# Nineteen weight chunks: high parts by rounding transfers of GpSimd's queue, low parts one chunk later, and ScalarE copying all transposed probabilities

## The reference

```python
h = rms_norm(x, norm1_g)
rx, rgate, q, kc, vc, ks, vs, kw, vw, nsa_g, mg_rnn, mg_attn = split(h @ w_in)
hr = rg_lru(causal_dwconv(rx, ...), ...)          # gated linear recurrence, two tanh gates
y_rnn = (hr * gelu(rgate)) @ w_rnn_out
y_attn = nsa(q, kc, vc, ks, vs, kw, vw, nsa_g, ...) @ w_attn_out   # three branches: compressed, selected, window
x = x + (sigmoid(mg_rnn) * y_rnn + sigmoid(mg_attn) * y_attn) @ w_out
```

## Time and profile before

| what | value |
|---|---|
| time, median of 3 runs | 812.38 us (812.19 to 812.41) |
| profiled execution, span | 810.6 us |
| PE busy | 799.6 us (99%) |
| DVE busy | 599.4 us (74%) |
| ACT busy | 487.0 us (60%) |
| POOL busy | 27.1 us (3%) |
| DMA | 143.79 MB, mean 177 GB/s |
| high parts by ACT (L629) | 127 of 1877 ns mean |
| low parts by DVE (L1074) | 127 of 2247 ns mean |

### The profile page before, as it was taken

How to read it: one execution, slowest core, us unless ns; L and a number is a source line. 1 busy time by engine, 2 the same in 40 slices (tenths; PEclk the granted TensorE clock), 3 DMA queues, 4 the chain that set the end, 5 groups by cost and what they waited for, 6 DMA issues and landing times.

```text
span 810.6 us, 11913 instructions
## 1 busy us (share of the span) xinstructions
PE 799.6 (99%) x4813; PEld 693.2 (86%) x4813; DVE 599.4 (74%) x773; ACT 487.0 (60%) x738; POOL 27.1 (3%) x38
## 2 busy tenths in 40 slices
PE   8999999999999999999999999999999999999996
PEld 7889998888888888988888888888888988888885
DVE  6774698998957986897878778877777665655556
ACT  6555598877757454765666566546755654544552
POOL 1102000000000000000000000020110000000000
PEclk9999999999999999999999999999999999999999
DMA  8446432342434674456455555764453655555441
GB/s 337 164 156 251 170 126 104 118 155 73 151 119 159 229 288 156 156 188 227 160 206 174 201 197 175 256 237 147 146 196 121 211 201 196 174 219 191 161 152 52
DMA packets 22630, 143.79 MB, mean 177 GB/s; under 512 B 2608, under 2 KB 3248, under 8 KB 8240
## 3 DMA queue, kind: packets, MB, share of 16 engines
q1 hardware_dynamic: 20880, 137.72, 48.3%
q10 hardware_dynamic: 1696, 5.31, 1.8%
HBM read 141.97 MB, written 1.05 MB: 176 GB/s over the span
## 4 chain that ended last, share of the span: by engine, by line
PE 93%; ACT 3%; DVE 2%; DMA 1%; issue 1%; DVEq 0%; SPq 0%; ACTq 0%
PE PS L1748 19%; PE PS L1752 10%; PE PS L1801 10%; PE PS L1802 10%; PE PS L1805 10%; PE PS L1735 5%; PE PS L1736 4%; PE PS L1740 4%; PE PS L2115 3%; PE PS L1764 2%; PE PS L2094 2%; PE PS L1858 1%; PE PS L1892 1%; PE PS L2119 1%; PE PS L1869 1%; PE PS L2065 1%
## 5 line engine op out<-in xcount | busy, mean ns | idle before, releaser
L1074 DVE TENSOR_TENSOR WL<-RAW,WH 128x2048 fp32r<-128x2048 f32 (+2 forms) x127 | 285.1, 2247 | 31.1 <-ACT WH L629 31.0
L629 ACT ACTIVATE WH<-RAW 128x2048 fp32r<-128x2048 f32 (+2 forms) x127 | 238.2, 1877 | 47.0 <-PE PS L1805 25.7
L1490 DVE TENSOR_TENSOR HLS<-PS,HLS 128x512 f32<-128x512 f32 x46 | 31.7, 689 | 92.7 <-ACT HLS L977 92.7
L1748 PE MATMUL PS<-CHL,WH 128*128 128x512 f32 x352 | 87.9, 392 | 0.0
L1735 PE MATMUL PS<-BHL,WH 128*126 128x256 f32 (+1 forms) x336 | 83.6, 287 | 0.0
L977 ACT ACTIVATE HLS<-PS 128x512 f32<-128x512 f32 x46 | 27.4, 595 | 90.7 <-PE PS L1752 86.3
L1736 PE MATMUL PS<-BHL,WH 128*126 128x256 f32 (+1 forms) x336 | 81.8, 282 | 0.0
L1748 PE MATMUL PS<-BHL,WH 128*128 128x512 f32 x320 | 79.9, 392 | 0.0
L1748 PEld LDWEIGHTS PS<-CHL,WH 128*128 128x128 f32 x352 | 63.9, 189 | 11.8
L1802 PE MATMUL PS<-WH,AHL 128*128 128x512 f32 x176 | 68.8, 391 | 0.0
L1801 PE MATMUL PS<-WH,AHL 128*128 128x512 f32 x176 | 68.7, 390 | 0.0
(11 more groups left out here) (313 smaller groups left out, 1311.1 us busy)
## 6 DMA issues: line engine op xcount, KB each, us to landing
RAW<-in_w_stream SPq DMA_DIRECT2D x108, 1024.0 KB, 4.8
RAW<-in_w_stream SPq DMA_DIRECT2D x11, 1008.0 KB, 4.9
RAW<-in_w_stream SPq DMA_DIRECT2D x8, 704.0 KB, 4.5
WF<-in_w_stream SPq DMA_DIRECT2D x2, 1024.0 KB, 5.4
LN<-in_ln ACTq DMA_DIRECT2D x2, 1024.0 KB, 5.2
WF<-in_w_stream SPq DMA_DIRECT2D x4, 294.0 KB, 3.6
X<-in_x SPq DMA_DIRECT2D x2, 512.0 KB, 4.2
RAW<-in_w_stream SPq DMA_DIRECT2D x2, 512.0 KB, 6.8
```

The costliest lines, as they stand in the source:

```text
L629: eng.activation(WH[:, c % NSLOT, 0:CHUNKS[c][2]], raw(c), ACT.Copy).then_inc(w_hi, 1)
L1074: eng.tensor_tensor(WL[:, c % NSLOT, 0:CHUNKS[c][2]], raw(c), f32(WH[:, c % NSLOT, 0:CHUNKS[c][2]]), ALU.subtract).then_inc(w_lo, 1)
L1490: eng.tensor_tensor(HLS[:, n % 4, :, :], PS[:, bank:bank + 2, 0:TOK], HLS[:, n % 4, :, :], ALU.add)\
L1748: eng.matmul(PS[:, bank, :], wh, HL[:, k, :, :].rearrange("p a t -> p (a t)"), start=(k == 0), stop=False)
```

## The change

Nineteen of the chunks that have two parts, from chunk 17 to chunk 39 (all but the "ri" chunks), form the list CAST. For these:

- POOL issues a transfer from HBM straight into the slot of WH; source and target differ in type (float32 and the rounded type), so the transfer rounds. It waits until PE has finished chunk c - 3, and until the transfer two before it has landed. Two semaphores in turn say that it landed. SP loads RAW as before, so these chunks are read from HBM twice.
- ACT no longer rounds them. PE and DVE wait for the transfer in place of ACT's semaphore (`wait_high`).
- DVE makes the low part of chunk c + 1 at the top of iteration c, behind the maxima and ahead of the unit's weights, where it made that of chunk c + 2 in mid-iteration. It also waits for RAW itself.
- ACT copies both PSUM banks of the transposed probabilities, in one instruction of 128 x 1024; DVE's `unit_pt` is gone, and one semaphore takes the place of two.
- In the feed-forward parts two sets of semaphores become one; what is waited for stays the same.

```diff
+CAST = [c for c in range(AT[("ri", 0)] + 1, AT[("ao", 3)] + 1) if CHUNKS[c][3]]
+HI_NO = [sum(1 for b in range(c) if CHUNKS[b][3] and b not in CAST) for c in range(NCH)]
...
+        def wait_high(eng, c):
+            if c in CAST:
+                n = CAST.index(c)
+                eng.wait_ge(wh_in[n % 2], 16 * (n // 2) + 16)
+            else:
+                eng.wait_ge(w_hi, HI_NO[c] + 1)
...
@@ gpsimd
             power(crs[0:NKV * CP, :], css[0:NKV * CP, :], 1, HD, EPS, kc_rstd)
+            for n, c in enumerate(CAST):
+                eng.wait_ge(chunk_done, c - NSLOT + 1)
+                if n >= 2:
+                    eng.wait_ge(wh_in[n % 2], 16 * (n // 2))
+                source = A_w[OFFS[c]:OFFS[c + 1]].rearrange("(p n) -> p n", p=P)
+                eng.dma_start(WH[:, c % NSLOT, 0:CHUNKS[c][2]], source).then_inc(wh_in[n % 2], 16)
@@ scalar, split
-                if c >= NCH or not CHUNKS[c][3]:
+                if c >= NCH or not CHUNKS[c][3] or c in CAST:
@@ scalar, unit_pt
-                eng.activation(PT[:, u % 2, 0, :, :].rearrange("p h q -> p (h q)"), PS[:, 4, :], ACT.Copy)\
-                   .then_inc(pt0_copied, 1)
+                eng.activation(PT[:, u % 2, :, :, :].rearrange("p a h q -> p (a h q)"),
+                               PS[:, 4:6, :].rearrange("p a q -> p (a q)"), ACT.Copy).then_inc(pt_copied, 1)
@@ vector, split
-                s = SPLIT_NO[c]
-                eng.wait_ge(w_hi, s + 1)
+                wait_high(eng, c)
+                if c in CAST:
+                    eng.wait_ge(raw_in[ARRIVAL[c][0]], 16 * (ARRIVAL[c][2] + 1))
@@ vector, window
-                u = unit_at(w - 2)
-                if u is not None:
-                    unit_pt(u)
@@ vector, loop over c
-                if c and CHUNKS[c - 1][0] == "ri" and c - 1 != SPLIT_AHEAD or c == UNIT_FIRST:
+                if c + 1 in CAST:
                     split(c + 1)
...
-                if CHUNKS[c][:2] not in SUMS_FIRST and kind != "ri" and c != W0 and c + 1 != UNIT_FIRST or c == SPLIT_AHEAD:
+                if CHUNKS[c][:2] not in SUMS_FIRST and c + 2 not in CAST and c != W0:
                     split(c + 2)
```

More of the change, by code:

```diff
@@ L437, in two_block_program @@
             "pct_done", "pct_copied", "qk_done", "nb_ready", "exp_done", "p_ready", "t_done"))
-        pt0_copied, pt1_copied, pv_done, o_hi, o_lo, rnn_g, la_ready = (sem(n) for n in (
-            "pt0_copied", "pt1_copied", "pv_done", "o_hi", "o_lo", "rnn_g", "la_ready"))
+        pt_copied, pv_done, o_hi, o_lo, rnn_g, la_ready = (sem(n) for n in (
+            "pt_copied", "pv_done", "o_hi", "o_lo", "rnn_g", "la_ready"))
         ix_ready, sq_ready, w_ready, root_ready, scan_ready, g_hi, g_lo, m_ready = (sem(n) for n in (
@@ L453, in two_block_program @@
             "mix_done", "os_ready", "os_ss", "os_rstd", "mr_ready", "mrt_done", "mrt_hi", "mrt_lo"))
[L454 to L457, removed]
+        y_mean, y_std, eps_ready, x0_low, y_ln, xt4_done, xt4_hi, xt4_lo = (sem(n) for n in (
+            "y_mean", "y_std", "eps_ready", "x0_low", "y_ln", "xt4_done", "xt4_hi", "xt4_lo"))
+        z_gain, wt_ready, rnn_in, xw_ready, gate_t_done, x_sq2 = (sem(n) for n in (
+            "z_gain", "wt_ready", "rnn_in", "xw_ready", "gate_t_done", "x_sq2"))
         half_copied, halves_summed = sem("half_copied"), sem("halves_summed")
+        wh_in = [sem("wh_in0"), sem("wh_in1")]
+        def wait_high(eng, c):
[4 more added lines that the diff above has]
+                eng.wait_ge(w_hi, HI_NO[c] + 1)
         def wait_tile(eng, c, t):
@@ L975, in half_copy @@
                 if n >= 4:
-                    eng.wait_ge(up_conv if n - 4 < N_UP else up2_prod, n - 3 if n - 4 < N_UP else n - 3 - N_UP)
+                    eng.wait_ge(up_conv if n - 4 < N_UP else up_prod, n - 3)
                 eng.activation(HLS[:, n % 4, :, :], PS[:, bank:bank + 2, TOK:2 * TOK], ACT.Copy).then_inc(half_copied, 1)
@@ L1002, in up2_silu_of @@
                 if i >= 4:
-                    eng.wait_ge(up2_lo, i - 3)
-                eng.activation(SG[:, i % 4, :], HLS[:, i % 4, 0, :], ACT.Silu).then_inc(up2_silu, 1)
+                    eng.wait_ge(up_lo, N_UP + i - 3)
+                eng.activation(SG[:, i % 4, :], HLS[:, i % 4, 0, :], ACT.Silu).then_inc(up_gelu, 1)
             def up2_first(i):
-                eng.wait_ge(up2_prod, i + 1)
+                eng.wait_ge(up_prod, N_UP + i + 1)
                 if i >= NA:
                     eng.wait_ge(chunk_done, AT["dn2", (i - NA) // 2] + 1)
-                eng.activation(AH[:, i % NA, :], SG[:, i % 4, :], ACT.Copy).then_inc(up2_hi, 1)
+                eng.activation(AH[:, i % NA, :], SG[:, i % 4, :], ACT.Copy).then_inc(up_hi, 1)
             def gained_hi(kp):
@@ L1113, in unit_weights @@
                    .then_inc(p_ready, 1)
[L1115 to L1120, removed]
             a_started = [0] * NG
@@ L1517, in up2_product @@
                 eng.wait_ge(halves_summed, N_UP + i + 1)
-                eng.wait_ge(up2_silu, i + 1)
+                eng.wait_ge(up_gelu, N_UP + i + 1)
                 eng.tensor_tensor(SG[:, i % 4, :], HLS[:, i % 4, 1, :], SG[:, i % 4, :], ALU.mult)\
-                   .then_inc(up2_prod, 1)
+                   .then_inc(up_prod, 1)
             def up2_second(i):
-                eng.wait_ge(up2_hi, i + 1)
+                eng.wait_ge(up_hi, N_UP + i + 1)
                 eng.tensor_tensor(AL[:, i % NA, :], SG[:, i % 4, :], f32(AH[:, i % NA, :]), ALU.subtract)\
-                   .then_inc(up2_lo, 1)
+                   .then_inc(up_lo, 1)
             def unit2_max(u):
@@ L1776, in tile0_under_norm @@
             def tile0_under_norm(banks, c, HL, lo_ready):
-                eng.wait_ge(w_hi, SPLIT_NO[c] + 1)
+                wait_high(eng, c)
                 for ks in (range(4), range(4, KD)):
@@ L1781, in tile0_under_norm @@
                         hl_high(banks[0] + v, c, 1024 * v, HL, 0, ks, lo_ready)
-                eng.wait_ge(w_hi, SPLIT_NO[c + 1] + 1)
+                wait_high(eng, c + 1)
                 for v in range(2):
@@ L1864, in unit_t @@
                 if u >= 1:
-                    eng.wait_ge(pt0_copied, u)
-                    eng.wait_ge(pt1_copied, u)
+                    eng.wait_ge(pt_copied, u)
                 for part in range(2):
@@ L1886, in unit_pv @@
                                    PC[:, g // 2, P * qt:P * qt + P], start=(pp == 0), stop=False, skip_group_check=True)
-                eng.wait_ge(pt0_copied, u + 1)
-                eng.wait_ge(pt1_copied, u + 1)
+                eng.wait_ge(pt_copied, u + 1)
                 for part in range(2):
@@ L2105, in main @@
                     if i < 2:
-                        eng.wait_ge(pt0_copied, NU)
-                        eng.wait_ge(pt1_copied, NU)
+                        eng.wait_ge(pt_copied, NU)
                     else:
@@ L2152, in main @@
                 if kind in ("dn", "dn2"):
-                    first_bank, lo_s, n_all = (2, up_lo, N_UP // 2) if kind == "dn" else (0, up2_lo, N_UP2 // 2)
+                    first_bank, before, n_all = (2, 0, N_UP // 2) if kind == "dn" else (0, N_UP, N_UP2 // 2)
                     def down_half(cc, j, t, n):
@@ L2158, in down_half @@
                                       j == 0, j == n_all - 1)
-                    eng.wait_ge(lo_s, 2 * i + 2)
+                    eng.wait_ge(up_lo, before + 2 * i + 2)
                     if i < n_all - 2:
@@ L2170, in main @@
                             down_half(c, i, 1, 0)
-                        eng.wait_ge(w_hi, SPLIT_NO[c + 1] + 1)
-                        eng.wait_ge(lo_s, 2 * i + 3)
-                        eng.wait_ge(up_hi if kind == "dn" else up2_hi, 2 * i + 4)
+                        wait_high(eng, c + 1)
+                        eng.wait_ge(up_lo, before + 2 * i + 3)
+                        eng.wait_ge(up_hi, before + 2 * i + 4)
                         s = (c + 1) % NSLOT
@@ L2188, in main @@
                             eng.matmul(outs[n], AH[:, units[1], 0:P], weights(WL, 1, n), start=False, stop=False)
-                        eng.wait_ge(lo_s, 2 * i + 4)
+                        eng.wait_ge(up_lo, before + 2 * i + 4)
                         for n in range(2):
@@ L2210, in main @@
                         for t, j in (((0, 0), (0, 1), (1, 0)), ((1, 1),))[i]:
-                            eng.wait_ge(w_hi, SPLIT_NO[c - i + j] + 1)
+                            wait_high(eng, c - i + j)
                             eng.wait_ge(xt3_lo, 4 * t + 2 * j + 2)
```

## The result

The changed kernel takes 813.40 us in the median (10 runs, from 813.22), the kernel before 812.37: 1.03 us more, a ratio of 1.0017 with a 95% interval of 1.0009 to 1.0025. The profiled execution has a span of 811.6 us against 810.6. The forecast was 813.9, and within its bound of 0.2% this is no change. One of the ten executions took 816.54 us, at a mean granted clock of 0.993; the others lie between 813.22 and 813.62.

The account below looks back on a forecast made before the run. PE, busy 799.6 of 810.6 us, was taken to bound the kernel. Plus 2.18 us at chunk 20 minus 0.62 of waits gives 1.56; 810.6 + 1.78 (median over profiled span) + 1.56 = 813.9 us, range 811.5 to 818.0.

Parts of the forecast that it names:

- its bound of 0.2%: Whole kernel: 810.8 to 814.0 us counts as no change; 0.2% is 1.6 us, about what a measurement can tell.
- The low parts: DVE, 101.55 to 120.47: three low parts instead of two make unit 1's maxima 1.97 us late; PE loses 2.18 at chunk 20.
- The copy: ACT: copying 1024 columns takes about 1.05 us, 0.44 more; it lies beside PE everywhere but at chunk 20.
- The wait on ACT's gate eviction: Chunk 20: one of the few waits that PE was said to have between 85 and 245 us before the change.
- The waits that go: PE at chunk 23 (0.52 us, behind chunk 24's rounding) and at the transposes of 164.77 (0.10): together minus 0.62 us.
- The transfers: POOL's queue: each takes 6.2 us (4.9 plus 1.3 for issuing), costing nothing even at chunk 18, the tightest place.
- The room of 7.5 us at chunk 18: From chunk 15's end, about 98.5, to DVE's need at 106.1; each us of transfer above 7.5 costs PE one.
- No later stretch gives it back.: PE behind chunk 20: the 2.18 us lost there stay lost, as the longest later wait is 0.5 us.
- the likeliest case: Whole kernel: the forecast case, chance 0.57, with 813.9 us and model errors of some 0.5: 813.4 to 814.4 us.
- The late transfer: Rival, chance 0.26: transfers over 7.5 us delay chunk 18, then the ao chunks; 814.9 us at 8.5, 824.3 at 12.7.
- carry bits over without rounding: Rival at the transfers: no rounding happens, low parts would be small or zero, time the same; no chance given.
- Not slower: Rival, chance 0.12: DVE makes up 1.5 us between 101.55 and 120.47, maxima ready by about 120.9; 811.8 us.

Follow-up runs that it names:

- e4: Changed kernel with sixteen chunks in CAST, from 21 on; ACT rounds 17, 18 and 19, low parts made as before the change: 811.37 us, ratio 0.9989 to the kernel before.
- e8: Changed kernel with sixteen chunks in CAST, from 21 on, and unit 0's copy alone divided between ACT and DVE again: 811.33 us, ratio 0.9988.
- e5: Changed kernel, but chunk 17 alone is rounded by ACT and has its low part in its old place: 812.69 us, ratio 1.0009.
- e1: Changed kernel, but DVE makes chunk 17's low part in the middle of iteration 15 again; its transfer stays: 813.41 us, ratio 1.0018.
- e2: Changed kernel with the copy of the transposed probabilities divided again, one bank on ACT and one on DVE, for all twelve units: 812.87 us, ratio 1.0008.
- e3: Kernel before the change, with only the copies changed: ACT copies both banks in one instruction, DVE none: 812.46 us, ratio 1.0001.
- e6: Changed kernel, but ACT rounds chunk 24, behind unit 3's exponentials, as before the change: 814.04 us, ratio 1.0027.
- e7: Changed kernel, but chunk 18's transfer waits for chunk 16's end in place of chunk 15's: 816.12 us median of 6 executions, ratio 1.0049.
- e9: Changed kernel, but its transfers declare one type at both ends: 813.39 us, ratio 1.0017.

## Why the prediction was right

**The low parts.** This was the term that was to decide, and it was the largest. The chain came as forecast, link by link: maxima at 122.34 (122.44 forecast), exponentials at 122.37 (122.55), the copy 1.04 us long (1.05), the third gate tile at 126.48 (126.68). PE's 2.00 us are the forecast's 2.18 less 0.10 of the maxima and 0.08 of the step from them to the exponentials (0.11 forecast, 0.03 measured). e4 and e8 take the three low parts back to their old places, and with them the loss goes to 0.14 and 0.00. What I had put too simply is the cause: e5 shows that taking one low part out of the run gives back 0.8 us only, since another must stand where DVE waits for unit 0's scores; and e1 that the old place is of no use to a high part that a transfer brings as late as 99.69.

**The copy.** 0.44 us at chunk 20, measured 0.42 (e2). It is 0.21 without the late maxima (e3), so it was rightly counted on top of them, not by itself. The wait on ACT's gate eviction that the prediction reads from the earlier trace rows isn't there: the rows show the tanh ahead of the third gate tile, and the list of waits has none at chunk 20 before the change. What hides 0.23 us of the copy is ACT's own wait for the gate tile (e3), not a pause of PE.

**The waits that go.** Minus 0.52 at chunk 23, measured 0.60, and e6 brings it back by chunk 24's rounding alone. Minus 0.10 at the transposes of 164.77, measured 0.11; there the reason was only half of it: either the copy on ACT (e3) or the low part moved behind DVE's copy (e2) takes that wait away.

**The transfers.** 6.2 us estimated, 5.2 measured in the median; the estimate added a POOL instruction of 1.3 us where issuing takes 0.54. The room of 7.5 us at chunk 18 was about right (issued at 98.92, asked for at 106.10): 5.1 us cost nothing, and in e7 each us past the asking time cost one. At the ao chunks PE waits for no transfer, though DVE waits 3.63 us for chunk 36's. SP's load of chunk 19 took 7.3 us and landed at 111.12 in place of 108.7, still ahead of DVE at 114.58. Where transfers are longest (7.5 us), SP loads beside them; chunk 17's took 8.0 us in e6 and e7, over the prediction's limit of 7.5, without harm, as there it is asked for only at 101.5.

**What failed.** "No later stretch gives it back." The ro chunks give back 0.23 us and the stretch up to 319 us another 0.08. I went by the longest wait in the list and passed over the pause at 281 us, where PE waits for DVE's mixing of an earlier ro chunk, as e3 still shows. In the kernel before it stands between these two rows:

```profile
279.48 1.47 PE L2119 MATMUL PS<-AHL,WL 126*128 126x256 f32 x11
281.06 2.31 PE L2115 MATMUL PS<-AHL,WH 126*128 126x512 f32 x9
```

Every run with transfers for the ao chunks lacks it. Likely it is because DVE no longer waits for ACT's rounding of chunk 39; no run took this by itself. The kernel before has this idle time ahead of DVE's low part, the one after has none on ACT's rounding there:

```profile
255.28 2.29 DVE L1074 TENSOR_TENSOR WL<-RAW,WH 128x2048 fp32r<-128x2048 f32 x1 [0.70 <-ACT WH L629]
```

Where the 0.08 comes from isn't shown. With it the sum of the table is -0.02 + 2.00 - 0.60 - 0.11 - 0.23 - 0.08 = 0.96 in place of 1.56, which is the 0.5 us between forecast and time to within 0.1. The mechanism was right, and the sum was 0.6 too large: 0.31 by this term, 0.18 at the gate tile, and 0.11 in the smaller ones. That the time came out as no change was close by the prediction's own count: 813.9 lay 0.1 us inside its bound of 814.0, and it gave 0.47 to no change and 0.48 to slower. The measured time lies at the lower end of the likeliest case, 813.4 to 814.4, because of the term that it had left out.

**The rivals.** The late transfer didn't happen; its place and its price at chunk 18 were right (e7), and its price at the ao chunks was not tested. That the transfers carry bits over without rounding was left open: no trace shows it (e9). "Not slower" needed DVE to catch up 1.5 us; its low parts took the same 2.25 us with ACT idle beside them, so what was put against it held.

## What to carry to other kernels

Where one engine is full, 36 us of work taken from another are worth only the waits that this work made: here 0.6 us, for one rounding of the nineteen, and a few tenths more. Moving a step later in a busy engine's order is a change of its own, and it is to be counted from the last idle time that it leaves behind to the next wait on the result; a step that fills a hole can't be moved without another one to fill it. The part of a change that helps can often be had without the part that hurts: the list begun three chunks later gives 811.37 us, 0.9 less than the kernel before in the same set of runs.

## What the runs showed of the hardware

- After waits of 2.1 and 0.5 us, PE's granted clock fell to half (0.50) from 127.4 to 130.8 us in the profiled execution of e1, and that cost 1.6 us. The same two waits in the profiled execution of e7 left the clock at full speed, while three other executions of it took 3 to 4 us more at a mean clock of 0.991 to 0.994. What decides between the two isn't shown.
- Shorter waits may do it too. Executions at 816 us and over, all with a mean clock of 0.991 to 0.994, come in the changed kernel (1 of 10; PE's waits at chunk 20 are 1.3 and 0.5 us in its trace), e9 (1 of 10) and e6 (1 of 6) with the same two waits, e5 (1 of 12; 0.5 and 0.5 us), e1 (2 of 12, beside the one above) and e7 (3 of 6). The kernel before has none (812.67 at most), nor have e2, e3, e4 and e8, whose traces show one wait there or none. There is no trace of any of these, so where the clock fell in them isn't shown.
- A transfer of 1 MiB from POOL's queue with a change of type takes 0.54 us of POOL and lands in 5.0 to 5.2 us when nothing moves beside it, about as SP's plain load (4.9). Beside one of SP's loads it took up to 8.1 us (e1), and 9.3 beside another transfer of its queue and one of SP's (e7).
- Where two overlap, in these traces it is mostly the later one that is stretched. In the changed kernel POOL's transfer of 102.10 took 5.1 us, and SP's load issued at 103.81, beside it, 7.3; SP's load of 206.12 took 4.7 us, and POOL's transfer of 206.28 took 7.5.
